# One core, hybrid attention trunk: values as the stationary operand with one accumulation per unit, and the causal mask added by VectorE together with the row maximum

## The reference

```
h = rmsnorm(x, norm_g[i]); proj = h @ w_in[i]
# A) forgetting attention, 8 heads x 64
s = q @ k.T * scale + c_q - c_k ; prob = softmax(where(causal, s, NEG)) ; o = prob @ v
# B) native sparse attention, 8 heads x 64 in 2 groups
o_cmp = softmax(q @ k_cmp.T) @ v_cmp      # 31 compressed keys
o_sel = softmax(q @ k_sel.T) @ v_sel      # at 512 tokens all 8 blocks are selected: plain causal
o_win = softmax(q @ k_win.T) @ v_win      # window 512: plain causal
o = g0 * o_cmp + g1 * o_sel + g2 * o_win  # sigmoid gates per token and head
# C) differential attention, 4 heads, two 64-d maps, 128-d values
w = prob0 - lam * prob1 ; o = rmsnorm(w @ v)
```

## Time and profile before

| | |
|---|---|
| median of three runs | 1657.7 us (1655.0 to 1657.88) |
| the profiled execution: its time, its span | 1655.21 us, 1653.4 us |
| TensorE busy | 1549.5 us, 94% of the span |
| weight loads | 1231.8 us, 74% |
| VectorE | 932.6 us, 56% |
| ScalarE | 627.2 us, 38% |
| GpSimd | 93.2 us, 6% |
| HBM | 73 GB/s over the span |
| granted TensorE clock, mean | 0.985 |

### The profile page before, as it was taken

One profiled execution on the slowest core, in us unless ns is written; L12 is line 12 of the kernel. 1 busy time (PEld: TensorE's weight loads), 2 busy tenths in 40 slices (PEclk: granted clock), 3 DMA queues, 4 the chain that ended last, 5 costly groups with the idle time before them and its releaser, 6 DMA issues. The chain is left out here.

```text
span 1653.4 us, 24216 instructions
## 1 busy us (share of the span) xinstructions
PE 1549.5 (94%) x8257; PEld 1231.8 (74%) x8257; DVE 932.6 (56%) x1907; ACT 627.2 (38%) x1479; POOL 93.2 (6%) x94
## 2 busy tenths in 40 slices
PE   3999999999999998999869999999999999899995
PEld 2777778787887776878647777777887877688774
DVE  6555665555547666454345556555555566755543
ACT  3333343333334433343334333333334444334333
POOL 2100000000000000000120000000000000000010
PEclk9999999999999999999969999999999999999998
DMA  4223242222223332332142233222222233233221
GB/s 132 77 64 96 77 109 52 67 62 53 69 64 90 90 83 57 98 113 67 48 114 78 66 99 98 71 60 64 57 66 72 68 90 84 64 96 101 83 82 51
DMA packets 249767, 129.58 MB, mean 78 GB/s; under 512 B 45658, under 2 KB 243892, under 8 KB 249652
## 3 DMA queue, kind: packets, MB, share of 16 engines
q1 hardware_dynamic: 249652, 128.13, 28.9%
HBM read 118.67 MB, written 2.10 MB: 73 GB/s over the span
## 5 line engine op out<-in xcount | busy, mean ns | idle before, releaser
L760 PE MATMUL D<-h_hi,w_hi 128*128 128x512 f32 x1264 | 547.5, 433 | 31.1 <-POOL h_lo L721 19.6
L762 PE MATMUL D<-h_lo,w_hi 128*128 128x512 f32 x1264 | 500.7, 396 | 0.0
L761 PE MATMUL D<-h_hi,w_lo 128*128 128x512 f32 x1264 | 499.0, 395 | 0.0
L1203 DVE TENSOR_TENSOR w_lo<-raw,w_hi 128x512 fp32r<-128x512 f32 (+2 forms) x508 | 298.7, 629 | 352.3 <-ACT w_hi L1015 352.1
L1015 ACT ACTIVATE w_hi<-raw 128x512 fp32r<-128x512 f32 (+2 forms) x508 | 268.4, 577 | 332.8 <-PE D L762 329.2
L760 PEld LDWEIGHTS D<-h_hi,w_hi 128*128 128x128 f32 x1264 | 240.8, 191 | 79.4 <-issue 15.4
L762 PEld LDWEIGHTS D<-h_lo,w_hi 128*128 128x128 f32 x1264 | 240.2, 190 | 54.3
L1107 ACT ACTIVATE probs<-S,nmax 128x128 f32<-128x128 f32 (+3 forms) x256 | 132.7, 523 | 374.8 <-DVE nmax L1359 374.8
L761 PEld LDWEIGHTS D<-h_hi,w_lo 128*128 128x128 f32 x1264 | 242.3, 192 | 29.9
L1359 DVE TENSOR_REDUCE nmax<-S 128x1 f32<-128x128 f32 (+3 forms) x256 | 113.2, 483 | 77.4 <-PE S L892 77.0
L904 PE MATMUL T<-ident,probs 128*128 128x128 f32 x560 | 98.6, 274 | 21.1 <-DVE probs L1372 15.1
(11 more groups left out here) (214 smaller groups left out, 1553.5 us busy)
## 6 DMA issues: line engine op xcount, KB each, us to landing
raw<-in_w_in_dram SPq DMA_DIRECT2D x124, 512.0 KB, 3.9
raw<-in_w_in_dram SPq DMA_DIRECT2D x32, 256.0 KB, 3.5
raw<-in_w_out_dram SPq DMA_DIRECT2D x16, 512.0 KB, 3.5
raw<-in_w_ple_gate_dram SPq DMA_DIRECT2D x16, 512.0 KB, 3.6
rs<-rx SPq DMA_DIRECT2D x80, 64.0 KB, 2.0
raw<-in_cmp_w_k_dram SPq DMA_DIRECT2D x8, 512.0 KB, 3.7
raw<-in_cmp_w_v_dram SPq DMA_DIRECT2D x8, 512.0 KB, 3.7
raw<-in_w_br_a_dram SPq DMA_DIRECT2D x16, 256.0 KB, 2.6
```

The costliest lines, as they stand in the source:

```text
L760: pe.matmul(o, w_hi[:, sl, cs], hi[:, k, :], start=(k == 0), stop=False)
L761: pe.matmul(o, w_lo[:, sl, cs], hi[:, k, :], start=False, stop=False)
L762: ins = pe.matmul(o, w_hi[:, sl, cs], lo[:, k, :], start=False, stop=last)
L1203: TT(w_lo[:, sl, half], raw[:, t % RAW, half], f(w_hi[:, sl, half]), ALU.subtract).then_inc(M["dve_lo"], 1)
```

## The change

**Values stationary.** For A and B the values are now the stationary operand and the probabilities the moving one. The values are split: the 128 stationary columns of a head are 64 of the high part and 64 of the rest (`va_st`, `v_b`). The transposed probabilities are split too: ScalarE writes the high part from PSUM (now for all rows of A and B), VectorE subtracts (L1461) and writes the rest. `pT` holds two query blocks (256 columns) for each head, each part and each key block. An item `V2` handles a pair of query blocks (c = 0: i = 0, 1; c = 1: i = 2, 3): for each key block one matmul with the high part and one with the rest, 256 columns, or 128 for the last key block: 4 matmuls for c = 0 and 8 for c = 1. The output has channels on partitions, so the transposes of `Y` go for A and B. For this the probabilities must be normalized first: item `SC` (one tick after `S`) takes the reciprocals, multiplies by the gates and scales the two rows of `probs`. Both chunks and, in B, both branches and the compressed one accumulate in one bank per head (`O0`, `O1`), which is read once per unit in `Y`: ScalarE copies one half of the partitions (high part or rest) over, VectorE adds the other.

**Mask.** The two mask matmuls go. VectorE adds a bf16 mask and takes the maximum in one `tensor_tensor_reduce`, which also writes the masked scores to `probs`. The exponential then works in `probs`, and the next `S` waits for the maximum (`dve_max`) and not for the exponential.

**What goes with it.** `T` stands two ticks after its row for A and B too, and there is one bank for transposes, so `T` waits for the copies of the `T` before. In a B unit the rows go by pairs of query blocks: sel 0, 1, win 0, 1, then sel 2, 3, win 2, 3. The tiles `va` 2 and 3, `ksb` and the `w1k` tiles stand elsewhere in stages 0 to 2. For room, `pT` lies over the residual `xT`: SyncE stores `xT` (2 MB) to `x_keep` in HBM at the start of a layer, behind the loads of tiles 0 to 5, and loads it back when all of `V` is done, ahead of the loads of `p` and of the tiles from the third `mgc` on. C keeps its float32 product with the probabilities stationary.

```diff
-                lag = 2 if branch(prob_rows[ti][0]) == "C" else 1
-                limit = tick - lag
-                while ti < len(prob_rows) and prob_rows[ti][4] <= limit:
+            if 0 < j <= len(rs) and j % 2 and branch(s) != "C":
+                parts.append(("SC", rs[j] - 1))
...
+            while ti < len(prob_rows) and prob_rows[ti][4] <= tick - 2:
+                parts.append(("T", ti))
+                u, i, m, h, _ = prob_rows[ti]
+                if m == "c":
+                    vq.append((tick + 1, ("V", ti)))
+                elif i % 2:
+                    vq.append((tick + 1, ("V2", vgroups.index((u, i // 2, m, h)))))
+                ti += 1
...
+        def copied(eng, k):
+            if k < KC:
+                eng.wait_ge(M["pt_lo_s"], k + 1)
+            else:
+                eng.wait_ge(M["ptc_s"], k - KC + 1)
+
+        def pair_block(k):
+            u, i, m, h, _ = prob_rows[k]
+            cols = slice((i % 2) * P, (i % 2) * P + P)
+            src = Tr[:, 0:(i + 1) * P].rearrange("p (j q) -> p j q", j=i + 1)
+            return pT[:, h, 0, 0:i + 1, cols], pT[:, h, 1, 0:i + 1, cols], src
...  SyncE
+                    sp.dma_start(x_keep, xT[:]).then_inc(M["xk_st"], 16)
...
                     sp.wait_ge(M["dve_ysplit"], 12)
+                    sp.wait_ge(M["pe_v"], len(prob_rows) - KC)
+                    sp.wait_ge(M["xk_st"], 16)
+                    sp.dma_start(xT[:], x_keep).then_inc(M["xk_ld"], 16)
                     sp.dma_start(p_tok, p[bass.ds(L, 1)].rearrange("a b (t p) c -> p (a b t) c", p=P)).then_inc(M["p_ld"], 16)
...  TensorE
                             if r >= 2:
-                                pe.wait_ge(M["act_exp"], r)
+                                pe.wait_ge(M["dve_max"], r)
...
-                            for h in range(2):
-                                pe.matmul(Sc[h][:, qs], identb[:], maskb[:], start=False, stop=True).then_inc(M["pe_s"], 1)
...  T
-                                pe.wait_ge(M["act_exp"], r + 1)
-                            if k >= 2:
-                                pt_wait(pe, k - 2)
+                                pe.wait_ge(M["dve_scale"], scales.after(r))
+                            if k:
+                                copied(pe, k - 1)
...
+                        elif what == "V2":
+                            u, c, m, h = vgroups[it[1]]
+                            copied(pe, prob_at[(u, 2 * c + 1, m, h)])
...
+                            for j in range(2 * c + 2):
+                                q0 = max(j - 2 * c, 0) * P
+                                v = va_st[:, u % 2, j, h * P:(h + 1) * P] if m == "a" else \
+                                    v_b[:, j, int(m == "win"), h * P:(h + 1) * P]
+                                for x_ in range(2):
+                                    ins = pe.matmul(Oh[h][:, 2 * c * P + q0:(2 * c + 2) * P], v, pT[:, h, x_, j, q0:2 * P],
+                                                    start=(first and j == 0 and x_ == 0),
+                                                    stop=(m == "a" and j == 2 * c + 1 and x_ == 1))
+                            if m == "win":
+                                pe.wait_ge(M["dve_misc"], misc.after(("ct", u)))
+                                ins = pe.matmul(Oh[h][:, 2 * c * P:(2 * c + 2) * P], vcmp[:, h, :],
+                                                pcT[:, 2 * c * P:(2 * c + 2) * P], start=False, stop=True)
...  ScalarE
+                            A(hi_, src, ACT.Copy).then_inc(M["pt_hi_s"], 1)
...  VectorE
-                                RED(nmax[:, r % 8:r % 8 + 1], Sc[r % 2][:, 0:n], AX.X, ALU.max,
-                                    negate=True).then_inc(M["dve_max"], 1)
+                                dve.tensor_tensor_reduce(probs[:, r % NP_, 0:n], Sc[r % 2][:, 0:n], maskb[:, S - n:S],
+                                                         -1.0, 3.0e38, ALU.add, ALU.min,
+                                                         nmax[:, r % 8:r % 8 + 1]).then_inc(M["dve_max"], 1)
+                        elif what == "SC":
...
+                            dve.wait_ge(M["act_exp"], r + 2)
+                            link(dve.reciprocal(pair, sums[:, u % 2, i, c:c + 2]))
+                            if m != "a":
+                                gv = gates[:, i, :].rearrange("p (g n b) -> p b g n", g=2, n=4)[:, c // 2, :, u - 4]
+                                link(TT(pair, pair, gv, ALU.mult))
+                            for h in range(2):
+                                pr = probs[:, (r + h) % NP_, 0:n]
+                                TS(pr, pr, pair[:, h:h + 1], None, ALU.mult).then_inc(M["dve_scale"], 1)
+                        elif what == "T":
...
+                                dve.wait_ge(M["pt_hi_s"], k + 1)
+                                TT(lo_, src, f(hi_), ALU.subtract).then_inc(M["pt_lo_s"], 1)
```

More of the change, by code:

```diff
@@ L238, in make_schedule @@
                 items.append(part)
[L239 removed]
+                if part[0] == "N":
                     follow.append([1, ("SQ", part[1])])
@@ L743, in _ @@
                 def _(pe):
-                    pe.matmul(Mb[:], ones[:], ssum[:], start=True, stop=True).then_inc(M["pe_norm"], 1)
+                    pe.matmul(Mb[:], ones[:].to_broadcast([P, P]), ssum[:], start=True, stop=True).then_inc(M["pe_norm"], 1)
                     pe.wait_ge(M["par_ld"], 64)
@@ L927, in _ @@
-                            if last and branch(u) == "B":
-                                if i == 0:
-                                    pe.wait_ge(M["dve_misc"], misc.after(("ct", u)))
-                                hs = slice(64 * (i % 2), 64 * (i % 2) + 64)
-                                ins = pe.matmul(Ob[:, 0:P], pcT[hs, i // 2, :], vbd[hs, :], start=True, stop=True)
+                                ins = pe.matmul(Ob[:, 0:P], pTc[:, (k - KC) % 2, j * P:(j + 1) * P],
+                                                vc_tok[:, j, (u - 8) * P:(u - 7) * P], start=(j == 0), stop=(j == i))
@@ L1431, in _ @@
                                ALU.mult).then_inc(M["yqc_s"], 1)
+                        elif what == "Y" and branch(it[1]) != "C":
+                            u = it[1]
+                            yf = y_f[:, y_slot(u), :]
+                            for h in range(2):
+                                ps = slice(HD * h, HD * h + HD)
+                                dve.wait_ge(M["act_fold"], 2 * u + h + 1)
+                                ins = TT(yf[ps], Oh[h][ps, :], yf[ps], ALU.add)
+                            ins.then_inc(M["fold_s"], 1)
+                            dve.wait_ge(M["fold_s"], u + 1)
+                            dve.wait_ge(M["dve_evac"], dve_evac.after(tile_of[("z" + branch(u).lower(), u % 4)]))
+                            STT(yf, yf, 0.5, zs[:], ALU.mult, ALU.mult).then_inc(M["yf_s"], 1)
                         elif what == "Y":
@@ L1509, in _ @@
             def _(pe):
-                pe.matmul(Mb[:], ones[:], ssum[:], start=True, stop=True).then_inc(o_pe, 1)
+                pe.matmul(Mb[:], ones[:].to_broadcast([P, P]), ssum[:], start=True, stop=True).then_inc(o_pe, 1)
                 for m in range(NM):
```

367 lines of the change are left out of this document (208 added, 159 removed).

## The result

The changed kernel takes 1703.6 us, median of 4 runs (1694.8 to 1704.3), beside 1657.2 (1655.0 to 1657.9) for the kernel before: a ratio of 1.0268, 95% interval 1.0251 to 1.0284. The profiled execution took 1703.13 us with a span of 1701.3. The prediction was 1611, so the change costs 46 us where it was to bring 47 (1657.7 to 1611).

A forecast was written before the change was run, and what follows sets the result against it. TensorE was taken to bound the kernel. 1655.2 (profiled) − 72.6 (stream) + 16 (B waits) + 2 (A) + 3 (C) + 5 (reload) = 1608.6; with the median 2.5 above the profiled execution, 1611 us, range 1584 to 1652.

The forecast's parts named there:

- Where TensorE will wait: New waits of TensorE, measured by the C units: 2 us per B unit, 16 in all; 2 for A; 3 for C.
- place (2): `T` needs the copies of the `T` before from one bank; `SC` waits for the second exponential; no size of its own.
- place (1): `V2` of head 0, second half of a B unit: two triples (1.4 us) against copy and subtraction, 1.4 us with engines free.
- Rival 3: VectorE and the hand-overs set the pace of B, 6 us per B unit (48): 1648 us, chance 0.17.
- The 84%: VectorE's forecast share of a B unit: 43.9 us of work in a unit that should take 52.2.
- TensorE's stream, −72.6: TensorE's stream gets 72.6 us shorter: 6.1 for each B unit, 2.6 for each A unit, 0.4 for each C unit.
- Rival 5: Values get no cheaper, short matmuls take 0.19 us each: 1651 us, chance 0.08.
- The mask, 12.8: Mask matmuls leaving TensorE: 128 pairs at 0.10 us save 12.8 us, or 24 if the switch costs 0.09 as well.
- The fused maximum: VectorE's masked maximum costs the plain one's 683 ns for 512 columns, plus a read-out of 0.16 us.
- Rival 4: Slower: the fused maximum takes twice the plain one, 10 us more per B unit: 1702 us, chance 0.10.
- C, +3: In C units the chain to `CB` gets two read-outs, so TensorE waits 3 us more than now.
- The reload, 5 us: Loading the stored residual back ahead of the third `mgc` tile comes late: 2.5 us per layer, 5 in all, up to 20.

The follow-up runs named there:

- the best version: Changed kernel with transposes of A and B first in their tick, three ticks after the scores, and `ct` in a B unit's fifth tick: 1625.8 us, ratio 0.981.

## Why the prediction was wrong

**The step that failed** is "For B I take 2 us per unit (ends 0 and 6), 16 in all; for A 2", under "Where TensorE will wait". Measured: 52.1 us at place (2) and 26.1 at place (1), 78 for 18; by branch 53.1 for the 16 of B and 24.9 for the 2 of A. On top of that comes a lower clock, which the sum put at nothing without a reason. The price of B was read from the C units, where a wait comes once per query block and for another reason; it said nothing of how many hand-overs a B tick has. The price of A rested on its ticks being half as dense. Both places were named rightly. Of the copy and the subtraction the text said that each "may be in a weight split or a maximum of 0.7", but no such term stood in the sum. In the window shown two halves of a weight split (1.16 us) and a tanh (0.58) stand ahead of ScalarE's copy, from 358.98 to 360.51, and so take nearly all the time that the two triples give.

**The cause.** The experiments bear out A and not B as I had them, though A's ranges were often missed: moving `T` to the front of its tick gave back 32 us, a tick more another 18, and `ct` out of the way 28 more, all with the same work. 31 us less work on VectorE changed no wait, and 84.6 us more cost 4 to 7 us while the hand-over from ScalarE went with it. Leaving out the rest gave back 58, which is chain and load together. Rival 3 said "VectorE and the hand-overs set the pace of B". The hand-overs do; that VectorE's load at 65% does not rests on the orders above, which change no work. The 84% that the text leaned on was not reached in unit 4.

**Where the loss stands, in unit 4.** From 58.30 us the stream takes off 5.3 (58.30 to the 52.98 of the same records at clock 1.00 in the best version); the lower clock puts 2.6 back (55.58 for 52.98); and TensorE is idle 8.6 us (64.20 less 55.58). 58.3 − 5.3 + 2.6 + 8.6 = 64.2. The 8.6 are the waits on L1461 (5.9 for `T`, 2.7 for `V2`).

**Point by point.**
- *TensorE's stream, −72.6*: near in its prices, somewhat too high. Value matmuls are 0.12 us apart for the 0.115 taken, and B unit 4 lost 5.3 us for 6.1. In the best version TensorE is busy 42.8 us less in B (48.8 forecast) and 15.3 less in A (20.8). The four B units of a layer take 224.8 us there (55.2, 53.4, 60.5, 55.7) after 239.2 before; the prediction's 6.1 less and 2 more each makes 222.8. The A units take 169.3 after 174.4, where the prediction makes 165. So for B the forecast was of the kernel with its waits covered. Rival 5 (0.19 each) is out.
- *The mask, 12.8*: out of the stream came 9.7 to 9.8 us, but it was not all gained: 3 us alone, nothing at three ticks, 5 beside covered waits, and a loss of 8 to 15 in the changed kernel. The way to the transposes did get longer: for 512 columns the maximum takes 688 ns and a read-out of 84 for 683 (VectorE), and the exponential, which now reads `probs` in SBUF and not the scores in PSUM, 716 for 683 (ScalarE). That this is what costs the 8 to 15 us is argued; no run isolates it.
- *The fused maximum*: 688 ns for 683, the lower end that I took. Rival 4's mechanism (twice the plain one) is wrong, though its time, 1702, is that of the result: a time that fits proves no cause. The Trainium skill, Vector Engine (DVE) Microarchitecture Reference, "Points that are easy to get wrong", says that two SBUF sources that aren't bf16 halve the rate of the two-source form with an accumulator. By that rule this form, with one source in PSUM and a bf16 mask, is spared, and the trace agrees (688 ns for 683); the slowed case itself is in no run here. The read-out is 0.084 us, half of the 0.16 assumed.
- *VectorE and ScalarE*: VectorE 1032.0 us for some 1070, unit 4 41.57 for 43.9: near enough. ScalarE 718.7 for 690: its new work is 91.5 us for the 63 forecast. The prediction left out its copies for `Y` (19.0 us, 32 of 0.593) and the longer exponentials (32 ns each, 256 of them: 8).
- *C, +3*: 43.50 us for 43.10 in unit 8, and 16.6 us of waits for combined maps for 15.1. Smaller than taken. In the best version unit 8 takes 45.8 us, with a new pause of 3.0 us ahead of a C value product that no experiment looked into.
- *The reload, 5 us*: 0. ScalarE waits 5.0 us a layer for the third `mgc` tile, as foreseen, but TensorE has work to cover it: from 674 us, where the merge begins, to 740 it waits for nothing but a tanh, for 1.0 us, as it did before.
- *Not in the sum*: the granted clock. Its mean is 0.957 for 0.985, some 146 us of the span at 1.2 GHz for 50 (the 0.043 and 0.015 that are missing, twice, times the span). Part of the new stretches lies ahead of the units of the first layer (10 to 60 us: 0.66 for 1.00); the best version has the same 0.66 there, so they are no part of what it gained. In A and B the clock is 0.96, 0.94, 0.99 and 0.97 in the windows above, for 0.99 in A and 1.00 in B before, and 0.98 and 1.00 in the best version.

Together, from the windows by branch, in us over both layers:

| | forecast | measured | off by | of it: TensorE idle | of it: TensorE busy |
|---|---|---|---|---|---|
| A units | −18.8 | +14.1 | 33 | 18 | 15 |
| B units | −32.8 | +26.0 | 59 | 37 | 22 |
| the rest | +4.8 | +7.8 | 3 | | |

In B the idle part is the waits on L1461; in A others are in it (5.4 us for `zs`), less what A waited before. The busy part has the lower clock and the stream in it: against the best version, whose records are the same, TensorE is busy 15.6 us more in B and 9.8 more in A, an estimate of what the clock cost; the other 11.5 are the stream, priced too high. In the best version the time is 15 us above the forecast with 24.8 us of `T` waits left.

## What to carry to other kernels

Before a copy out of a shared bank is put on two engines in turn, write down what stands ahead of it in each engine's order, its waits included, and compare that sum with the TensorE instructions up to the next use of the bank; engines at 60% say nothing about it. Where a change makes TensorE's stream cheaper and its hand-overs more, try it with the hand-overs a tick further apart before it is judged: the same work gave 1703.6 and 1625.8 us. And an instruction that waits for a late event must not stand ahead of one that TensorE will need sooner.

## What the runs showed of the hardware

A wait of TensorE in the middle of an otherwise full stage can be followed by a lower clock. In unit 1 of the second layer `T` waits 4.27 us; here VectorE is in L1339 (3.00 us) and L1345 (1.23), and ScalarE in L1102 between them, which waited 3.75 for the first; all of these stand ahead of the copy and the rest. TensorE around it, and the windows ahead of it and behind:

```profile
932.68 0.39 PE L779 MATMUL D<-h_hi,w_hi 128*128 128x512 f32 x1
932.91 0.39 PE L780 MATMUL D<-h_hi,w_lo 128*128 128x512 f32 x1
933.13 0.39 PE L781 MATMUL D<-h_lo,w_hi 128*128 128x512 f32 x1
937.79 0.87 PE L924 MATMUL T<-ident,probs 128*128 128x128 f32 x3 [4.27 <-DVE pT L1461]
...
938.89 0.63 PE L780 MATMUL D<-h_hi,w_lo 128*128 128x512 f32 x1
939.32 0.63 PE L781 MATMUL D<-h_lo,w_hi 128*128 128x512 f32 x1
```

```profile
925.00:937.00 12.00, 8.52 (x44) 6.20 (x42) 7.29 (x17) 4.38 (x9) 0.00 (x0) 1.00 0.31 87
937.00:947.00 10.00, 9.21 (x31) 7.11 (x31) 4.45 (x13) 3.00 (x8) 0.00 (x0) 0.50 0.12 28
```

The matmuls of a triple start 0.43 us apart for 0.23, and the granted clock is 0.50 (1.2 GHz) for the 10 us behind the wait: some 5 us lost beside the 4.27, by estimate. So a stall in a full stage can have a second price that its wait doesn't show.

How high this price is does not follow from the wait's length alone. The same wait in the first layer, 4.30 us, has only 3.6 us of it behind, and waits of 1.5 to 3.0 us in A and B of the same trace have mostly 3 to 4 us. The second line here is behind the wait of 2.95 us in unit 4:

```profile
110.60:114.20 3.60, 3.56 (x11) 2.91 (x12) 1.44 (x3) 0.49 (x1) 0.00 (x0) 0.55 0.00 0
275.40:278.50 3.10, 3.02 (x9) 2.52 (x10) 1.49 (x9) 1.15 (x5) 0.00 (x0) 0.55 0.00 0
```

On the other side, waits of 1.50 and 1.55 us (338.1 and 460.7) have none, nor has a pause of 3.01 us in the best version (495.1, its clock 1.00 to 502). In the best version units 4 and 7 stay at 1.00.

The second fact is a small one: ScalarE's exponential takes some 32 ns more in its new form, which reads `probs` in SBUF with a scale of −1, than reading the scores in PSUM. It is the same at every width: 715, 609, 502 and 394 ns for 512, 384, 256 and 128 columns with the mask part alone, for 683, 576, 469 and 362 before. No run parts the source from the scale.
